# Two transformer blocks on one core: attention heads moved in among the memory's projections, the memory's norm moved ahead of a gated unit's second half, two weight splits shared with ScalarE

## The chip, the cores and the metric

One Trainium2 chip, one core of it. The metric is the device time of one execution in microseconds. A core has a matrix engine (TensorE, PE in the profile, with its weight loads as PEld), VectorE (DVE), ScalarE (ACT), GpSimd (POOL) and SyncE (SP), which here issues the transfers of the weights. Each engine runs its own list of instructions in order, and semaphores tie the lists together.

## The reference, cut to what matters

`x` is 256 tokens of width 1024. A first model of two layers is followed by a second one of two layers. Only the first one's layers are touched:

```python
for l in range(2):
    h = rmsnorm(x, norm_mix[l])
    ... = split(h @ w_in[l])
    y_ssm = s5_mixer(...)      # z = gelu(y) @ w_glu: z_out * sigmoid(z_gate)
    y_mla = mla_mixer(...)     # 8 causal heads, q and k of 64+32, v of 64; then @ mla_w_o
    y_hg  = hgrn2_mixer(...)   # 4 heads, norm, gate; then @ hg_w_o
    merged = gate0 * y_ssm + gate1 * y_mla + gate2 * y_hg
    x = x + merged @ w_out[l]
    x = x + memory_cross_attention(rmsnorm(x, norm_cross[l]), rmsnorm(mem, norm_mem[l]),
                                   x_w_q[l], x_w_kv[l], x_w_o[l])
    x = x + swiglu_ffn(rmsnorm(x, norm_ffn[l]), ...)
```

`mem` is 256 rows of width 1024 and doesn't depend on `x`. Its norm and its projections `x_w_kv` (512 columns of keys, 512 of values) can run anywhere before the cross attention.

## The kernel before

The program is written as one function per engine, each a list in order. Two things set the order around the change: TensorE's list, and the transfers of weights, which SyncE issues in the order in which TensorE asks for chunks.

*Weights in chunks.* `chunk` stands for 512 KB of a weight matrix (128 partitions x 1024 fp32). Raw chunks land in a ring `W` of four slots (`RSLOTS`), and the transfer of chunk n waits for the release of chunk n - 4. Where a product is done in split precision (`product`, L400, three products of high and low parts for one), a chunk needs a high part `WH` and a low part `WL`, in rings of three slots (`HSLOTS`). A part written for split m waits until TensorE has used split m - 3. The word `low` says who makes them: with "dve" ScalarE makes the high part and VectorE the low part, with "pool" ScalarE the high part and POOL the low part, with "both" POOL makes the one after the other (`both_parts`). Inputs of such a product are split too (`HTH` and `HTL`, for `hg_w_o` `oHG`).

*Who makes splits when.* `split_to(n)` on an engine makes its parts of all splits below n that it has not made. `split_before[name]` is the number of splits that TensorE has asked for when it ends the group of that name; `ahead(name)` is that number and up to two more (`AHEAD`), as far as the raw ring allows. Evictions (`evict`, `high_of`, `low_of`, `row_max`) call it before they wait for their bank, so that weights are made ahead.

*Banks.* A group of products has one of 8 PSUM banks (`begin`, `end`), dealt out in turn, those of open groups left out. The next user of a bank waits until an engine has freed it (`free_after`).

*The stretch of the change in TensorE's list, in each layer.* The second half of the gated unit, `glu(1)`: groups `("glu", l, 1, 1, tt)`, the gate, and `("glu", l, 1, 0, tt)`, each of a plain and a split chunk. The transposes of `HV` (`hoT`). The transposes of the memory's scaled rows, `norm_T(nrm, memX)`. The product `yh` with `hg_w_o`, four wide chunks. The projections `ck` (keys, four chunks of 24 products of 256 columns) and `cv` (values, four of 12 products of 512 columns). Then the heads: turn h of eleven does the scores of head h (L585), the transposes of the probabilities of head h - 2 (L593) and the product with the values of head h - 3 (L871). Then `ym` with `mla_w_o`, in unsplit fp32, the transposes of `merged`, and `wo` with `w_out`.

*The other engines there.* ScalarE squares `ho`, evicts `qT`, does `glu_gate(1)` (the sigmoid), waits for `mem`, sums its squares (`norm_sums`), scales one half of the rows (`norm_rows`), makes the high halves of `hoT` and of the normalized memory (`norm_cols`), evicts `ck` and `cv`, and then does the heads' exponentials (`exps`, L1587) and evictions. VectorE makes `ho_ready`, does both tiles of `glu_out(1)` (product with the gate, product with `gates`: L2510, L2511), scales the other half of the memory's rows (L2038), makes low halves (L2143, L2064), `add_branch("yh")` (L2548, L2549), and then the heads' scale and mask, row maximum and division. POOL splits weights, loads `mem` (`load_mem`, L1362), and takes the norm's root (`norm_rstd`, L1298 and L1299), which both `norm_rows` wait for:

```python
split_to(split_before["glu", l, 1, 0, 1])
wait_full(pool, ("ho", l, 1))
load_mem()
split_to(split_before["glu", l, 1, 0, 1] + 1)
norm_rstd(nrm, halves=False)
```

`memX` (the memory's rows), `memSq` (their squares) and the tiles of the `hgrn2` levels share one buffer `TB`: `memX` may be loaded once level 8 has been multiplied, `memSq` written once `ho` has been.

Of the kernel before, what the change touches and what calls it, by code (L numbers as in the profile page):

```python
# [28 lines left out]
TT = S // P  # L29
DM = 1024  # L30
KT = DM // P
# [10 lines left out]
QD = NOPE + ROPE  # L42
HGH = 4
XH = 4
DFF = 2816
FT = DFF // P
THETA = 10000.0
# [19 lines left out]
def build(nc, T, out):  # L67

    with ExitStack() as ctx:
# [261 lines left out]
        def _(pe):  # L331
# [104 lines left out]
            def wide_steps(tag, wname, l, act, K, low="dve", after=None, at=0):  # L436

                ps = {(tt, h): begin(*tag, tt, h) for tt in range(TT) for h in range(2)}
                for k in range(K if after is None else K - 2):
                    n, w = chunk(tag, rows(wname, l, k, 1, 0, DM), 1, DM, low)  # L440
                    need_rows(act, k + 1)
                    for tt in range(TT):
                        for h in range(2):
                            m = product(ps[tt, h][:, :], act, w,
                                        lambda a: a[:, at + k, tt * P:tt * P + P],
                                        lambda b: b[:, 0, h * 512:h * 512 + 512], k == 0, k == K - 1)
                            if k == K - 1:
                                end(m, *tag, tt, h)
                    if k == K - 1:
                        release_with(n, (*tag, 1, 1))  # L450
                    else:
                        release(n, m)
                    yield
                if after is not None:
                    yield from last_two(tag, wname, l, act, K, ps, after, low, lambda k: at + k,
                                        lambda k: need_rows(act, k + 1))
# [66 lines left out]
            def feature_steps(tag, wname, l, act, K, c0, tiles, low="dve", kstep=2, extra=0):  # L523
# [3 lines left out]
                if extra:  # L527
                    kr = begin(*tag, "kr")
                for k0 in range(0, K, kstep):
                    n, w = chunk(tag, rows(wname, l, k0, kstep, c0, cols), kstep, cols, low)  # L530
                    need_rows(act, k0 + kstep)
                    last = k0 + kstep == K
                    for j in range(tiles):
# [159 lines left out]
            for l in range(DEPTH):  # L693
# [161 lines left out]
                norm_T(nrm, memX)  # L855
                for j in range(2):
                    freed("hoT", l, j)
                token_out_wide(("yh", l), "hg_w_o", l, oHG, 4, low="both")

                input_from("hT", nrm)  # L860
                nrm += 1
                feature_out(("ck", l), "x_w_kv", l, HT, KT, 0, 4, low="pool")
                token_out(("cv", l), "x_w_kv", l, HT, KT, 512, 512, low="pool")

                def mla_pv(h):
                    freed("mla", "t", (l, h))
# [6 lines left out]
                    if h % 2 == 1:  # L873
                        end(m, "mo", l, h // 2)

                for h in range(HEADS + 3):
                    if h < HEADS:
                        freed("qT", l, h // 2)
                        freed("kT", l, h // 2)
                        scores("mla", (l, h), qTm[0:QD, h, :], kTm[0:QD, h, :])  # L880
                    if 2 <= h < HEADS + 2:
                        pe.wait_ge(sem["probs"], probs_at["mla", l, h - 2])
                        probs_T("mla", (l, h - 2))
# [366 lines left out]
        def _(pool):  # L1250
# [114 lines left out]
            for l in range(DEPTH):  # L1365
# [17 lines left out]
                split_to(split_before["gate", l, 5, 1])  # L1383
                pool.wait_ge(sem["y_ready"], 4 * (l + 1))
                signal(halves_of(glu_half, UT, 2), "glu_halves", l + 1)
                split_to(split_before["glu", l, 1, 0, 1])
                wait_full(pool, ("ho", l, 1))
                load_mem()
                split_to(split_before["glu", l, 1, 0, 1] + 1)
                norm_rstd(nrm, halves=False)  # L1390
                nrm += 1
                split_to(split_before["cv", l, 1])
# [40 lines left out]
        def _(act):  # L1433
# [249 lines left out]
            for l in range(DEPTH):  # L1683
# [143 lines left out]
                    ins = act.activation(PB[:, tt * 512:tt * 512 + 512], bank(("ho", l, tt))[:, :], ACT.Square)  # L1827
                    signal(ins, "ho_sq", 2 * l + tt + 1)
                take_T("qT", qTm)
                glu_gate(1)  # L1830
                act.wait_ge(sem["mem_rows"], 16 * (l + 1))
                norm_sums(nrm, memX, memSq)
                norm_rows(nrm, memX, memX)
                for j in range(2):
                    high_of(2 * j, 2, "hoT", l, j, dst=oHG[0])
                norm_cols(nrm, "norm_mem", l)
                nrm += 1
                for j in range(2):
                    evict(two(ckT, j), "ck", l, j)
                for tt in range(TT):  # L1840
                    evict(cv[:, tt, :], "cv", l, tt)
                for h in range(HEADS + 3):
                    if h < HEADS:
                        exps("mla", (l, h), h)
                    if 2 <= h < HEADS + 2:
                        take_PT("mla", (l, h - 2), h - 2)
                    if h >= 4 and h % 2 == 0:
                        evict(oML[:, (h - 4) // 2, :], "mo", l, (h - 4) // 2, width=S)
                for j in range(4):
                    high_of(2 * j, 2, "mg", l, j)  # L1850
                norm_in(nrm, "norm_cross", l, ("wo", l))
# [151 lines left out]
        def _(dve):  # L2003
# [364 lines left out]
            for l in range(DEPTH):  # L2368
# [132 lines left out]
                for q in range(4):  # L2501
                    full("y", l, q)

                def glu_out(h):
                    for tt in range(TT):
                        cols = slice(h * 512, h * 512 + 512)
                        wait_freed(dve, ("glu", l, h, 1, tt))
                        name = ("glu", l, h, 0, tt)
# [17 lines left out]
                for tt in range(TT):  # L2526
# [4 lines left out]
                    free_after(tt_(o, bank(("ho", l, tt))[:, :].rearrange("p (h e) -> p h e", h=HGH), r, ALU.mult),  # L2531
                               "ho", l, tt)
                    signal(tt_(HV[:, tt, :], HV[:, tt, :], HG[:, tt, :], ALU.mult), "ho_ready", 2 * l + tt + 1)
                glu_out(1)
                norm_rows(nrm, memX, memX)
                for j in range(2):
                    low_of(2 * j, 2, "hoT", l, j, dst=oHG)
                norm_cols(nrm, "norm_mem", l)
                nrm += 1

# [240 lines left out]
```

## Time and profile before

| what | value |
|---|---|
| median of 3 runs | 1920.4 us (1919.24 to 1921.8) |
| the profiled execution | 1917.89 us, its span 1916.1 us |
| TensorE busy | 1804.5 us, 94% of the span |
| VectorE, ScalarE, POOL busy | 1232.3, 867.0, 277.2 us |
| mean granted TensorE clock | 0.979 of full |
| DMA | 274.61 MB, 143 GB/s on average |

Times in rows are in microseconds from the start of the span. A row for a stretch gives its ends, its length, then the busy us of PE, PEld, DVE, ACT and POOL, each with its number of instructions. Each engine's busy time is a share of the same span, and an engine that is busy 94% may still wait at places. The granted clock says which part of full speed the chip let TensorE have.

### The profile page before, as it was taken

What the parts mean: (1) busy time and instruction counts of PE and PEld (TensorE: products, weight loads), DVE (VectorE), ACT (ScalarE), POOL (GpSimd) and SP (SyncE); (2) the same over time, 40 slices, a digit from 0 to 9 for tenths busy, and PEclk for the clock granted to TensorE, in tenths of its full rate; (3) what the DMA queues carried; (4) which work ended last, traced back from release to release, by engine and by line L of the source; (5) the groups of instructions that cost most, each with busy time, mean ns of one, the idle gap of its engine ahead of it and who ended that gap; (6) DMA issues with size and microseconds to landing.
All of it is one profiled execution on the core that took longest, in us unless ns stands there. A gap on an engine that the chain in (4) does not pass through costs nothing.

```text
span 1916.1 us, 27084 instructions
## 1 busy us (share of the span) xinstructions
PE 1804.5 (94%) x10038; PEld 1446.3 (75%) x10038; DVE 1232.3 (64%) x1895; ACT 867.0 (45%) x1413; POOL 277.2 (14%) x274
## 2 busy tenths in 40 slices
PE   7999989989999999999888999998899999989998
PEld 6676667569998866677577998656799864779987
DVE  7996755445667893855455566565677645566775
ACT  4224444355444422444355445336555543555553
POOL 4015453020000003557012000100100000010000
PEclk9999999999999999999999999998999999799999
DMA  6444442436566444445054666431455644135554
GB/s 160 130 130 152 133 152 89 143 105 180 160 187 188 119 127 142 133 133 177 28 191 116 194 184 192 147 110 56 141 177 163 193 153 121 56 107 170 169 187 138
DMA packets 192359, 274.61 MB, mean 143 GB/s; under 512 B 25616, under 2 KB 129540, under 8 KB 192228
## 3 DMA queue, kind: packets, MB, share of 16 engines
q1 hardware_dynamic: 191364, 269.86, 46.2%
q0 software_dynamic: 864, 3.02, 0.6%
q8 instruction: 80, 1.31, 0.3%
q14 instruction: 51, 0.42, 0.1%
HBM read 271.78 MB, written 1.05 MB: 142 GB/s over the span
## 4 chain that ended last, share of the span: by engine, by line
PE 80%; DVE 7%; ACT 6%; issue 3%; SPq 1%; POOL 1%; DMA 1%; DVEq 0%; ACTq 0%; POOLq 0%
PE bank L400 46%; PE bank L398 23%; DVE WL L1165 2%; ACT WH L1452 2%; PE bank L671 1%; PE bank L585 1%; PE bank L593 1%; PE bank L1021 1%; PE bank L871 1%; PE bank L1041 1%; PE bank L488 1%; ACT HTH L1452 1%; DVE bank L2117 1%; POOL WL L1165 0%; PE bank L654 0%
## 5 line engine op out<-in xcount | busy, mean ns | idle before, releaser
L1165 DVE TENSOR_TENSOR WL<-W,WH 128x1024 fp32r<-128x1024 f32 x304 | 372.5, 1225 | 241.9 <-ACT WH L1452 233.0
L1452 ACT ACTIVATE WH<-W 128x1024 fp32r<-128x1024 f32 x328 | 347.5, 1059 | 302.3 <-PE bank L400 267.2
L400 PE MATMUL bank<-HTH,WH 128*128 128x256 f32 x1536 | 437.6, 285 | 19.6 <-DVE WL L1165 9.5
L400 PE MATMUL bank<-HTL,WH 128*128 128x256 f32 x1536 | 434.5, 283 | 0.0
L400 PE MATMUL bank<-HTH,WL 128*128 128x256 f32 x1536 | 434.5, 283 | 0.0
L400 PEld LDWEIGHTS bank<-HTH,WH 128*128 128x128 f32 x1536 | 294.5, 192 | 25.2 <-DVE WL L1165 11.8
L400 PEld LDWEIGHTS bank<-HTL,WH 128*128 128x128 f32 x1536 | 294.7, 192 | 0.1
L400 PEld LDWEIGHTS bank<-HTH,WL 128*128 128x128 f32 x1536 | 294.6, 192 | 0.0
L400 PE MATMUL bank<-WH,HTL 128*128 128x512 f32 x672 | 261.4, 406 | 0.0
L400 PE MATMUL bank<-WH,HTH 128*128 128x512 f32 x480 | 192.7, 402 | 18.5 <-POOL WL L1165 5.7
L400 PE MATMUL bank<-WL,HTH 128*128 128x512 f32 x480 | 188.5, 393 | 0.0
L398 PE MATMUL bank<-W,M 128*128 128x512 f32 (+1 forms) x416 | 166.2, 555 | 2.6 <-issue 2.6
L400 PEld LDWEIGHTS bank<-WH,HTL 128*128 128x128 f32 x672 | 127.1, 189 | 32.2 <-issue 5.3
L398 PE MATMUL bank<-W,HTF 128*128 128x512 f32 (+1 forms) x384 | 149.8, 539 | 0.0
L398 PEld LDWEIGHTS bank<-W,M 128*128 128x128 f32 x416 | 79.2, 194 | 75.7 <-issue 72.9
L400 PEld LDWEIGHTS bank<-WH,HTH 128*128 128x128 f32 x480 | 91.2, 190 | 43.8 <-POOL WL L1165 7.4
L398 PEld LDWEIGHTS bank<-W,HTF 128*128 128x128 f32 x384 | 68.2, 190 | 67.5 <-issue 66.1
L1293 POOL TENSOR_SCALAR QSQ<-QSQ 128x2 f32<-128x2 f32 x9 | 5.1, 571 | 767.4 <-ACT PB L1492 767.4
L400 PEld LDWEIGHTS bank<-WL,HTH 128*128 128x128 f32 x480 | 91.2, 190 | 18.1
L398 PE MATMUL bank<-HTF,W 128*128 128x256 f32 x448 | 99.6, 381 | 0.7 <-DVE HTF L2392 0.6
L1338 POOL TENSOR_TENSOR WL<-W,WH 128x1024 fp32r<-128x1024 f32 x40 | 97.6, 2440 | 3.2
L398 PEld LDWEIGHTS bank<-HTF,W 128*128 128x128 f32 x448 | 84.3, 190 | 13.4 <-issue 1.4
(405 smaller groups left out, 2495.8 us busy)
## 6 DMA issues: line engine op xcount, KB each, us to landing
W<-in_w_in SPq DMA_DIRECT2D x132, 512.0 KB, 3.7
W<-in_ffn_w_gate_up SPq DMA_DIRECT2D x176, 256.0 KB, 3.4
W<-in_w_up SPq DMA_DIRECT2D x176, 256.0 KB, 3.6
W<-in_ffn_w_down SPq DMA_DIRECT2D x44, 512.0 KB, 3.7
W<-in_w_down SPq DMA_DIRECT2D x44, 512.0 KB, 4.2
W<-in_w_out SPq DMA_DIRECT2D x32, 512.0 KB, 3.4
W<-in_ssm_w_glu SPq DMA_DIRECT2D x16, 512.0 KB, 4.3
W<-in_x_w_kv SPq DMA_DIRECT2D x16, 512.0 KB, 3.4
```

Of the source, the lines that this page charges most:

```text
L398: return pe.matmul(out, at_a(a), at_b(b), start=start, stop=stop, skip_group_check=True)
L400: m = pe.matmul(out, at_a(a[x]), at_b(b[y]), start=(start and i == 0), stop=(stop and i == 2), skip_group_check=True)
L488: m = pe.transpose(ps[:, k * S + tt * P:k * S + tt * P + P], X[:, tt, (2 * j + k) * P:(2 * j + k) * P + P], IDENT[:, :])
L585: ins = pe.matmul(ps[:, tt * S:tt * S + S], qT[:, tt * P:tt * P + P], kT, start=(tt == 0), stop=(tt == TT - 1), skip_group_check=True)
L593: ins = pe.transpose(ps[:, kt * S + tt * P:kt * S + tt * P + P], p_buf(tag, m[1])[:, tt, kt * P:kt * P + P], IDENT[:, :])
L671: m = pe.matmul(ps[:, h * P:h * P + P], ka[:, h, b * P:b * P + P], qa[:, h, b * P:b * P + P], start=(h == 0), stop=(h == HGH - 1), skip_gr ...
L871: m = pe.matmul(ps[64 * (h % 2):64 * (h % 2) + 64, 0:S], vtok[:, kt, h * VD:h * VD + VD], PT[h % 2][:, kt, :], start=(kt == 0), stop=(kt = ...
L1021: pe.matmul(ps[:, tt * S:tt * S + S], qkT[r:r + 64, h // 2, tt * P:tt * P + P], qkT[r:r + 64, 4 + h // 4, :], start=(tt == 0), stop=False, ...
L1041: m = pe.matmul(ps[:, h * HD:h * HD + HD], t_buf("a2", h)[:, kt, tt * P:tt * P + P], proj2[:, kt, 640 + (h // 4) * HD:640 + (h // 4) * HD ...
L1165: eng.tensor_tensor(WL[:, m % HSLOTS, 0:width], W[:, n % RSLOTS, 0:width], h, ALU.subtract)\
L1338: signal(pool.tensor_tensor(low, raw, high.bitcast(F32), ALU.subtract), s, v)
L1452: copy = lambda dst, src, scale=1.0: act.activation(dst, src, ACT.Copy, scale=scale)
```

## The change

Three edits, the same in both layers of the first model.

1. *The heads.* TensorE's `ck` and `cv` steps are made one iterator `memory` of eight chunks. Two run ahead of the heads, the other six in turns 0, 1, 3, 5, 7 and 9 (`MEM_STEPS`), behind that turn's scores. ScalarE evicts `ck` in turn 1 behind the exponentials and `cv` behind the last turn, and asks for its parts of the splits ahead of each head's exponentials. The first two `ck` chunks get their low parts from VectorE instead of POOL.
2. *The memory's norm.* POOL loads `mem` when level 8 is done, ahead of the split of the (1, 0) chunk, and takes the root ahead of the first `hg_w_o` chunk. ScalarE sums the squares ahead of `glu_gate(1)`. VectorE scales its rows ahead of `glu_out(1)` and makes the low halves of `hoT` between that one's two tiles.
3. *The splits of `hg_w_o`.* Of the last two of the four chunks ScalarE makes the high part, one behind the first four columns of the memory's high halves and one behind the last four.

```diff
+MEM_STEPS = (0, 1, 3, 5, 7, 9)
...
# TensorE
-                token_out_wide(("yh", l), "hg_w_o", l, oHG, 4, low="both")
+                token_out_wide(("yh", l), "hg_w_o", l, oHG, 4, low=("both", "both", "pool", "pool"))
...
-                feature_out(("ck", l), "x_w_kv", l, HT, KT, 0, 4, low="pool")
-                token_out(("cv", l), "x_w_kv", l, HT, KT, 512, 512, low="pool")
+                memory = itertools.chain(feature_steps(("ck", l), "x_w_kv", l, HT, KT, 0, 4,
+                                                       low=("dve", "dve", "pool", "pool")),
+                                         token_steps(("cv", l), "x_w_kv", l, HT, KT, 512, 512, low="pool"))
...
+                next(memory)
+                next(memory)
                 for h in range(HEADS + 3):
                     if h < HEADS:
                         ...
                         scores("mla", (l, h), qTm[0:QD, h, :], kTm[0:QD, h, :])
+                    if h in MEM_STEPS:
+                        next(memory)
# POOL
-                split_to(split_before["glu", l, 1, 0, 1])
-                wait_full(pool, ("ho", l, 1))
-                load_mem()
-                split_to(split_before["glu", l, 1, 0, 1] + 1)
+                split_to(split_before["glu", l, 1, 1, 1])
+                wait_full(pool, ("lev", l, 8, 0))
+                load_mem()
+                split_to(split_before["glu", l, 1, 0, 1])
                 norm_rstd(nrm, halves=False)
# ScalarE
-                glu_gate(1)
                 act.wait_ge(sem["mem_rows"], 16 * (l + 1))
                 norm_sums(nrm, memX, memSq)
+                glu_gate(1)
                 norm_rows(nrm, memX, memX)
                 for j in range(2):
                     high_of(2 * j, 2, "hoT", l, j, dst=oHG[0])
-                norm_cols(nrm, "norm_mem", l)
+                last_yh = split_before["yh", l, 1, 1]
+                high_cols(nrm, "norm_mem", l, 0, 4)
+                split_to(last_yh - 1)
+                high_cols(nrm, "norm_mem", l, 4, KT)
+                split_to(last_yh)
                 nrm += 1
-                for j in range(2):
-                    evict(two(ckT, j), "ck", l, j)
-                for tt in range(TT):
-                    evict(cv[:, tt, :], "cv", l, tt)
                 for h in range(HEADS + 3):
                     if h < HEADS:
+                        split_to(ahead(("mla", "s", (l, h))))
                         exps("mla", (l, h), h)
+                    if h == MEM_STEPS[1]:
+                        for j in range(2):
+                            evict(two(ckT, j), "ck", l, j)
                     ...
+                for tt in range(TT):
+                    evict(cv[:, tt, :], "cv", l, tt)
# VectorE
-                glu_out(1)
                 norm_rows(nrm, memX, memX)
+                glu_out(1, (0,))
                 for j in range(2):
                     low_of(2 * j, 2, "hoT", l, j, dst=oHG)
+                glu_out(1, (1,))
                 norm_cols(nrm, "norm_mem", l)
```

`glu_out` takes the tiles it is to do as a second argument, and `wide_steps` and `feature_steps` take a tuple for `low`, one word a chunk.

## Rows read from the trace of the kernel before

**Rows 1.** the page's busy times: engine, us, share, instructions

```profile
PE 1804.5 (94%) x10038; PEld 1446.3 (75%) x10038; DVE 1232.3 (64%) x1895; ACT 867.0 (45%) x1413; POOL 277.2 (14%) x274
```

**Rows 2.** stretches of layers 0 and 1: length, busy us (count), clock, DMA share, GB/s

```profile
267.80:277.48 9.68, 4.92 (x26) 4.30 (x25) 9.40 (x9) 4.91 (x10) 7.12 (x4) 0.71 0.60 213
277.48:288.90 11.42, 11.42 (x49) 9.35 (x48) 5.09 (x9) 3.29 (x5) 7.07 (x4) 0.94 0.22 67
288.90:311.48 22.58, 22.58 (x146) 20.69 (x145) 9.99 (x7) 8.16 (x9) 15.71 (x7) 1.00 0.56 184
311.48:340.19 28.71, 22.94 (x96) 14.10 (x96) 18.00 (x40) 17.81 (x46) 0.00 (x0) 0.88 0.00 1
...
873.80:881.20 7.40, 3.93 (x26) 3.34 (x25) 7.16 (x8) 4.52 (x9) 7.17 (x4) 0.89 0.63 229
881.20:915.50 34.30, 34.30 (x194) 30.25 (x194) 15.15 (x16) 11.95 (x15) 23.07 (x11) 0.97 0.49 154
915.50:944.27 28.77, 22.99 (x96) 14.20 (x96) 18.00 (x40) 17.81 (x46) 0.00 (x0) 0.88 0.00 0
```

**Rows 3.** TensorE's timeline, layer 0: start, us, line, operation, tiles, count, idle before

```profile
248.68 1.06 PE L677 MATMUL bank<-TB 128*128 128x128 f32 x8
...
267.81 1.03 PE L689 MATMUL bank<-IDENT,HV 128*128 128x128 f32 x8
273.04 1.94 PE L564 MATMUL bank<-IDENT,TB 128*128 128x128 f32 x8 [4.20 <-issue]
```

**Rows 4.** VectorE's timeline, layer 0, and one row of layer 1

```profile
266.74 0.69 DVE L2510 TENSOR_TENSOR XN<-bank,PB 128x512 f32<-128x512 f32 x1 [5.46 <-PE bank L400]
267.47 1.54 DVE L2511 TENSOR_TENSOR XN<-XN,A 128x512 f32<-128x512 f32 x1
...
271.80 3.63 DVE L2038 TENSOR_SCALAR TB<-TB,RSTD 128x512 f32<-128x512 f32 x2
...
873.47 0.69 DVE L2511 TENSOR_TENSOR XN<-XN,A 128x512 f32<-128x512 f32 x1
```

**Rows 5.** ScalarE's timeline, layer 0

```profile
260.54 0.60 ACT L1553 ACTIVATE PB<-bank 128x512 f32<-128x512 f32 x1 [3.49 <-PE bank L400]
...
262.55 1.06 ACT L1482 ACTIVATE TB<-TB 128x1024 f32<-128x1024 f32 x1
...
267.45 1.48 ACT L1452 ACTIVATE TB<-TB,RSTD 128x512 f32<-128x512 f32 x2 [2.57 <-POOL RSTD L1299]
...
283.74 1.06 ACT L1452 ACTIVATE WH<-W 128x1024 fp32r<-128x1024 f32 x1 [5.02 <-PE bank L400]
```

**Rows 6.** POOL's timeline, layer 0, and the transfer of `mem`: KB, us to landing

```profile
254.50 0.97 POOL L1362 DMA_DIRECT2D TB<-in_mem  x1 [1.36 <-PE bank L825]
262.71 1.03 POOL L1336 CAST WH<-W 128x1024 fp32r<-128x1024 f32 x1 [7.24 <-DMA W<-in_hg_w_o]
263.83 2.38 POOL L1338 TENSOR_TENSOR WL<-W,WH 128x1024 fp32r<-128x1024 f32 x1
...
266.62 0.73 POOL L1299 TENSOR_TENSOR RSTD<-SSQ,NHALF 128x2 f32<-128x2 f32 x1
...
TB<-in_mem POOLq DMA_DIRECT2D x1, 1024.0 KB, 5.6
```

**Rows 7.** TensorE in the heads: its longest wait, two turns' scores

```profile
PE bank L593 <- DVE PB L2203: 3.5, 1, 3.5
...
323.08 1.15 PE L585 MATMUL bank<-TB 96*128 96x256 f32 x4
...
325.61 1.13 PE L585 MATMUL bank<-TB 96*128 96x256 f32 x4
```

**Rows 8.** ScalarE's first exponential; VectorE's sums from 281 to 300, by form

```profile
313.95 1.28 ACT L1587 ACT_TABLE_LOAD   x1 [1.78 <-DVE NMX L2191]
315.25 0.51 ACT L1587 ACTIVATE PB<-PB,NMX 128x256 f32<-128x256 f32 x1
...
L2549 DVE TENSOR_TENSOR XN<-XN,A 128x512 f32<-128x512 f32 x4 | 9.0, 2244 | 0.1
```

More of the change, by code:

```diff
@@ L439, in wide_steps @@
                 for k in range(K if after is None else K - 2):
-                    n, w = chunk(tag, rows(wname, l, k, 1, 0, DM), 1, DM, low)
+                    n, w = chunk(tag, rows(wname, l, k, 1, 0, DM), 1, DM,
+                                 low[k] if isinstance(low, tuple) else low)
                     need_rows(act, k + 1)
@@ L529, in feature_steps @@
                 for k0 in range(0, K, kstep):
-                    n, w = chunk(tag, rows(wname, l, k0, kstep, c0, cols), kstep, cols, low)
+                    n, w = chunk(tag, rows(wname, l, k0, kstep, c0, cols), kstep, cols,
+                                 low[k0 // kstep] if isinstance(low, tuple) else low)
                     need_rows(act, k0 + kstep)
@@ L2502, in _, with glu_out @@
                     full("y", l, q)
-                def glu_out(h):
-                    for tt in range(TT):
+                def glu_out(h, tts=range(TT)):
+                    for tt in tts:
                         cols = slice(h * 512, h * 512 + 512)
```

## The prediction

> **What bounds the kernel now.** I read the page first. TensorE is busy for 94% of the span [rows 1], so time can only come from places where it stands or runs at half clock, or from fewer products; the change removes no product. Then I cut the stretch that the diff touches into stages [rows 2]. There are two such stretches, one a layer. In each, TensorE is busy for 4.92 of 9.68 us (layer 0) and 3.93 of 7.40 us (layer 1) between the gated unit and the `hg_w_o` product, is full through the `hg_w_o` product and the memory's projections, and is busy for 22.94 of 28.71 us and 22.99 of 28.77 us in the eight attention heads. There its granted clock is 0.88 on average, a mixture of the 2.4 GHz and the 1.2 GHz level. Those two holes are what the change works on.
>
> *The first hole.* TensorE ends the transposes of `hoT` at 268.8 and does the first transposes of `memX` at 273.04 [rows 3]. It waits for the scaled rows of the memory. Working back: VectorE scales its half only from 271.80 on, in 3.63 us, because both tiles of `glu_out(1)` stand ahead of it [rows 4]. ScalarE scales its half at 267.45, having waited 2.57 us for POOL's root at 266.62 to 267.35 [rows 5, 6]. That root stands on POOL behind the 3.5 us split of the first `hg_w_o` chunk [rows 6], and the sums behind it start only at 262.55, after `glu_gate(1)` [rows 5].
>
> *The second hole.* With nothing but heads on TensorE, a head's scores wait for VectorE's row maximum, ScalarE's exponentials and VectorE's division. The first division alone holds TensorE for 3.5 us [rows 7]. Where nothing waits and the clock is full, one head's turn is 325.61 - 323.08 = 2.53 us [rows 7]. Eight are 20.2 us, against 28.7 us taken.
>
> **The change, part by part.** All against the profiled execution: 1917.89 us, of which the span is 1916.1. The median shown is 1920.4, or 2.5 above it, and I add that at the end.
>
> *Memory's norm earlier.* POOL issues the load of `mem` after level 8 (TensorE does it from 248.68 to 249.7 [rows 3]) and ahead of one more chunk's split instead of at 254.50. POOL has finished the (1,1) chunk's split by then. The issue takes 0.97 us [rows 6], so the (1,0) chunk's split ends about 1 us later, near 254.3. Its reader on TensorE comes some 3 us before the 267.81 of `hoT`, so this is hidden. The transfer takes 5.6 us [rows 6]: it is there at about 256. ScalarE comes to the sums when `qT` is evicted, at 260.54 - 3.49 = 257.05, and does them in 267.45 - 2.57 - 262.55 = 2.3 us [rows 5]. `glu_gate(1)` behind them is not late, its bank is full at 260.5. POOL's root is then ready at about 260.4, in front of the `hg_w_o` split, which begins when its data lands at 262.71 [rows 6]. VectorE, idle from 266.74 - 5.46 = 261.3 [rows 4], scales its rows until about 263, ScalarE after the gate until 264.1. Both are done before TensorE reaches the transposes at 268.8. These end at 268.8 + 1.8 = 270.5, sixteen at the pace of the eight of `hoT`, 0.11 each [rows 3].
>
> *What is late next.* The `hg_w_o` product needs the low half of `hoT` and a bank that `glu_out(1)`'s second tile frees. VectorE: first tile 0.69, its product with the gates 1.54 (as now, POOL splitting beside it), two low halves 0.7 each as other 128x512 operations, then 0.69 for the bank [rows 4]. From 266.74 this ends at 271.1; with semaphores 271.3, where TensorE starts the product now at 277.48. Layer 1's VectorE does its first product with the gates at 873.47 instead of 267.47, 606.0 later [rows 4], so the start is 877.3 instead of 881.2. At full clock the product is 11.42 x 0.94 = 10.7; I take 10.9. It ends at 282.2 instead of 288.9: 6.7 us in layer 0. In layer 1 the same way 3.9, and 0.3 for its clock of 0.97 instead of 1.00 over the first part: 4.2.
>
> *Do the splits keep up?* ScalarE now makes the high halves of `yh` chunks 2 and 3. A high half takes 1.06 us, a low half on POOL 2.38 [rows 5, 6], against 3.5 on POOL alone for both. By ScalarE's order (two `hoT` halves until 269.8, four columns of 0.5 us, since 128x1024 takes 1.06, then the high half) chunk 2's high half is ready at 272.9 and its low half at 275.3. TensorE wants it at 271.3 + 2 x 10.9 / 4 = 276.8. Chunk 3: 276.0, 278.4, wanted at 279.5. Each has about 1 us in hand. Chunks 0 and 1 of `ck` are split by ScalarE and VectorE by 279.2 and 281.9, wanted at 282.2 and 285.1. No stall, little slack.
>
> *Heads among the projections.* The eight projection chunks took 22.58 us [rows 2], 2.82 each, and stay. Two run before the first head, six inside the eleven turns. TensorE's load from the end of `yh` is 22.6 + 20.2 (heads at 2.53) + 0.8 for the eviction of the last output, as now. Waits: the first head's chain starts on VectorE with `add_branch("yh")`. Today it takes 4 x (0.69 + 2.24) = 12 us with the gaps, since its sum of two SBUF tiles takes 2.24 us beside POOL's splits [rows 8]; such an operation takes 0.69 without [rows 4]. From 282.0 the new one meets two of POOL's splits, not four, and I get 290.9. Row maximum 1.4 (two operations on 128x512), table load and exponentials 1.28 + 1.25 (two of 0.51 with their sums) [rows 8], one high half, the second head's exponentials, another high half, two evictions of `ck`: 299.2. The evictions free the bank in which `cv` begins. TensorE stands there from about 298.1: 1.1 us. After that a head's chain (maximum 1.4, exponentials 1.25, division 0.9, eviction 0.6) has two turns and a projection step, some 7.9 us, to run in. The high halves are asked for two chunks ahead. I see no further wait.
> So 282.2 + 22.6 + 20.2 + 0.8 + 1.1 = 326.9, where `ym` starts at 340.19 now: 13.3 us in layer 0. The middle alone is 51.3 - 44.7 = 6.6. In layer 1: 4.2 + 6.6 = 10.8.
>
> *The rest.* The `cv` evictions move behind the last head (1.2 us of ScalarE under `ym`'s 11.4), the fourth `ym` bank is one of them and is wanted last: nothing. The `w_out` transfer behind `ym` waits for `ym`'s own releases as before: nothing gained or lost.
>
> **Sum.** 13.3 + 10.8 = 24.1 less. I take 23, since several steps have under 1 us in hand. 1917.9 - 23 = 1894.9, and with the 2.5: **1897.4 us**. Its own range is 1889 to 1904: at best no wait and TensorE straight from the transposes into `yh`, 2 x (1.1 + 0.9) + 24.1 = 28 and 3 more for heads whose loads overlap the projections; at worst `add_branch("yh")` keeps its 12 us, 3 us a layer on the chain, and one us more.
>
> **Two rules.** The row of the table load shows 1.28 us and the exponential 0.02 us behind it, ScalarE having been idle [rows 8]. The Trainium skill, ScalarE: Activation LUTs, What ACT_TABLE_LOAD costs, gives about 1.38 us of drain besides for each change of set. By the row nothing is to be added; by the page `cv` would begin 1.4 us later in each layer, and the sum would be 21.3. The trace does not bear it out.
> The Trainium skill, SBUF — State Buffer, Who interferes with whom, speaks against this change: a VectorE operation with two SBUF inputs and a GpSimd operation fully block each other. The trace agrees, with the 2.24 against 0.69 us above. The third rival is what it would do to the heads.
>
> **The rivals.**
> 1. *Only the front gains* (chance 0.10). The heads' chain is the limit with or without company, each step of TensorE waits for it, and the eleven turns take the 51.3 us that they and the projections take now. Then 6.7 + 4.2 = 10.9 less: 1909.5. For it: the heads use 17.8 us of ScalarE and 18.0 of VectorE in 28.7 [rows 2], and ScalarE gets highs and evictions besides. Against: loads of both engines are under 80% of 44.7.
> 2. *Only the heads gain* (0.07). The memory's sums come late, because `mem` lands late or the root waits, and TensorE starts `yh` when it does now. 2 x 6.6 = 13.2 less: 1907.2. Against: the load has 1 us in hand at 256, and 5 more before the transposes.
> 3. *VectorE blocked by POOL in the heads* (0.11). Divisions and sums now run beside the four low halves of `cv`. Scaling rows of 128x512 took 3.63 for two beside POOL [rows 4]. At most each low half blocks for its whole 2.4 us on the path: 4 x 2.4 = 9.6 a layer, so 24.1 - 19.2 = 4.9 less, 1915.5; half of that is likelier, 1906. Against: division has several us in hand after the second head.
> 4. *A ring of waits, slower* (0.05). ScalarE's highs stand behind exponentials, these wait for maxima, these for scores, which TensorE does only behind the step that needs the high. If the two chunks ahead did not cover it, each step would pay scores 0.9, maximum 1.4, exponentials 1.25, high 1.06, low 2.4, step 2.8 = 9.8. The two `ck` steps have 5.3 of TensorE's own work in that time, the four `cv` steps 7.9, so 2 x 4.5 + 4 x 1.9 = 16.6 more a layer. 44.7 + 16.6 is 10.0 above the 51.3, so 20.0 slower less 10.9: 9 us slower, 1929. It decides from 12 us of stalls a layer on. Against it: the order written for ScalarE asks two ahead, and the raw chunks come early.
> The likeliest case keeps 0.67.
>
> **The range and the chances.** 1889 to 1910 takes in the likeliest, rivals 1 and 2 and the milder half of 3, with under 2 in 10 outside. Within 0.2% (3.8 us) is what a measurement can't tell from no change. Faster 0.92; the same 0.03 (the far end of rival 3); slower 0.05.
>
> **What would show it.** In the profile after: POOL's root before its first `hg_w_o` split; under 1.5 us between the `hoT` and the `memX` transposes' end and the product, no 4 us hole; the two `yh` chunks' highs on ScalarE and `yh` at an even 2.73 us a chunk; clock 1.00 through the heads; `add_branch("yh")` in about 9 us; one wait of about 1 us at the first `cv` step; 45 us from the end of `yh` to `ym`. It would be wrong if TensorE's waits for divisions or for low halves inside the turns came to more than 3 us a layer, or if a stage behind `ym` took longer than before.

## The result, and the profile after

The changed kernel takes 1896.87 us (median of 4 runs, 1893.49 to 1899.83) against 1919.82 for the kernel before (median of 4). The ratio is 0.9888, with a 95% interval of 0.9872 to 0.9903: 23 us less. The forecast was 1897.4. The execution that was profiled is the slowest of the four, 1899.83 us.

The page's busy times of the changed kernel, as [rows 1]:

```profile
PE 1798.9 (95%) x10038; PEld 1445.6 (76%) x10038; DVE 1233.6 (65%) x1899; ACT 872.4 (46%) x1417; POOL 264.2 (14%) x266
```

The two stretches of the changed kernel, cut at the same events as [rows 2]: from the transposes of `hoT` to the start of `yh`, to the end of `yh`, to the start of `ym`; the first three rows are layer 0, the others layer 1.

```profile
267.39:271.24 3.85, 2.78 (x25) 2.56 (x24) 2.68 (x5) 3.00 (x6) 2.56 (x1) 1.00 0.87 310
271.24:282.25 11.01, 11.01 (x49) 9.09 (x49) 6.75 (x12) 6.26 (x9) 4.82 (x2) 1.00 0.52 162
282.25:327.50 45.25, 42.62 (x241) 33.35 (x240) 29.75 (x48) 25.07 (x54) 14.28 (x6) 1.00 0.27 88
862.91:867.97 5.06, 2.79 (x26) 2.57 (x24) 4.92 (x5) 4.15 (x7) 2.02 (x1) 1.00 0.87 300
867.97:880.54 12.57, 12.57 (x48) 10.25 (x49) 6.50 (x11) 5.09 (x7) 4.91 (x2) 0.86 0.37 112
880.54:925.90 45.36, 42.36 (x241) 33.42 (x240) 29.68 (x49) 25.23 (x54) 14.30 (x6) 1.00 0.27 89
```

The reader is to see three things. The last stretch of each layer, projections and heads together, fell from 51.3 us (22.58 + 28.71, [rows 2]) to 45.25 and 45.36, and its clock is 1.00 throughout where the heads had 0.88. The front of layer 0, from `hoT` to the end of `yh`, fell from 288.90 - 267.81 = 21.09 to 14.86. The front of layer 1 fell only from 19.10 (873.81 to 892.91) to 17.63, and the clock of its `yh` is 0.86.

What held layer 1's front: VectorE's timeline, then POOL's, then TensorE's, of the changed kernel.

```profile
862.57 2.90 DVE L2530 TENSOR_TENSOR XN<-XN,A 128x512 f32<-128x512 f32 x1
...
866.96 0.69 DVE L2529 TENSOR_TENSOR XN<-bank,PB 128x512 f32<-128x512 f32 x1
```

```profile
862.55 2.38 POOL L1348 TENSOR_TENSOR WL<-W,WH 128x1024 fp32r<-128x1024 f32 x1
```

```profile
867.97 0.47 PE L401 MATMUL bank<-WH,OTR 128*128 128x512 f32 x1 [2.27 <-DVE XN L2529]
```

VectorE's product with the gates started 0.02 us behind POOL's difference and took 2.90 us. The low halves of `hoT` and the freeing of the second bank stood behind it, and TensorE idled 2.27 us and then ran part of `yh` at the lower clock. Of the 2.77 us by which this front is longer than layer 0's, 1.21 is the later start (5.06 against 3.85) and 1.56 the lower clock (12.57 against 11.01).

In layer 0 the same two operations came in the other order, VectorE's first, and VectorE's took 0.69 us. It then waited 1.06 us for ScalarE's high half of `hoT` all the same:

```profile
267.03 0.69 DVE L2530 TENSOR_TENSOR XN<-XN,A 128x512 f32<-128x512 f32 x1
268.78 1.42 DVE L2162 TENSOR_TENSOR OTR<-bank,OTR 128x512 fp32r<-128x512 f32 x2 [1.06 <-ACT OTR L1462]
```

```profile
267.23 2.73 POOL L1348 TENSOR_TENSOR WL<-W,WH 128x1024 fp32r<-128x1024 f32 x1
```

What waits of TensorE's are left in layer 0's stretch (engine and line that waited, releaser, us in total, times, longest), against the 3.5 us of [rows 7] and the 4.20 us of [rows 3]:

```profile
PE bank L401 <- ACT M L1563: 1.2, 1, 1.2
...
PE bank L401 <- issue: 1.1, 1, 1.1
PE bank L399 <- issue: 0.8, 1, 0.8
PE bank L875 <- ACT PB L1563: 0.7, 1, 0.7
```

The first is the eviction of `ck` ahead of the first `cv` step, the second the start of `yh`, the third the last output before `ym`, the fourth an eviction of transposed probabilities.

### The profile page after: what moved, and what is told of

Its sections match the earlier page's. It is cut to its first block, busy times and chain, and to the rows that moved or that the text cites. A ratio compares the mean times of both kernels' runs of the same rounds, so it can differ in the third digit from the quotient of the medians.

```text
span 1898.0 us, 27088 instructions
## 1 busy us (share of the span) xinstructions
PE 1798.9 (95%) x10038; PEld 1445.6 (76%) x10038; DVE 1233.6 (65%) x1899; ACT 872.4 (46%) x1417; POOL 264.2 (14%) x266
## 4 chain that ended last, share of the span: by engine, by line
PE 81%; DVE 8%; ACT 5%; issue 2%; SPq 1%; POOL 1%; DMA 0%; DVEq 0%; ACTq 0%; POOLq 0%
PE bank L401 47%; PE bank L399 24%; DVE WL L1175 2%; ACT WH L1462 2%; PE bank L674 2%; PE bank L588 1%; PE bank L596 1%; PE bank L1031 1%; PE bank L875 1%; PE bank L1051 1%; PE bank L490 1%; ACT HTH L1462 1%; DVE bank L2136 1%; DVE HTL L2083 1%; POOL WL L1175 1%
## 5 line engine op out<-in xcount | busy, mean ns | idle before, releaser
L1175 DVE TENSOR_TENSOR WL<-W,WH 128x1024 fp32r<-128x1024 f32 x308 | 377.5, 1226 | 254.0 <-ACT WH L1462 245.2
L1462 ACT ACTIVATE WH<-W 128x1024 fp32r<-128x1024 f32 x332 | 352.3, 1061 | 288.7 <-PE bank L401 255.6
L401 PE MATMUL bank<-WH,HTH 128*128 128x512 f32 x480 | 194.7, 406 | 21.1 <-POOL WL L1175 5.7
L401 PEld LDWEIGHTS bank<-WL,HTH 128*128 128x128 f32 x480 | 91.8, 191 | 18.1
L1348 POOL TENSOR_TENSOR WL<-W,WH 128x1024 fp32r<-128x1024 f32 x36 | 87.9, 2441 | 2.9
```

What stands on the lines that cost most here:

```text
L401: m = pe.matmul(out, at_a(a[x]), at_b(b[y]), start=(start and i == 0), stop=(stop and i == 2), skip_group_check=True)
L1175: eng.tensor_tensor(WL[:, m % HSLOTS, 0:width], W[:, n % RSLOTS, 0:width], h, ALU.subtract)\
L1348: signal(pool.tensor_tensor(low, raw, high.bitcast(F32), ALU.subtract), s, v)
L1462: copy = lambda dst, src, scale=1.0: act.activation(dst, src, ACT.Copy, scale=scale)
```

## The experiments

Each kernel was timed beside the kernel before in five rounds. Since runs of one kernel spread over up to 13 us (e7), the stretches of the traces say more than the ratios. Two lengths are used throughout: the *front*, from the first transpose of `hoT` to the end of `yh`, and the *middle*, from there to the start of `ym`, each for both layers. For the kernel before they are 21.1 and 19.1, and 51.3 and 51.4; for the changed kernel 14.9 and 17.6, and 45.3 and 45.4.

**e1_heads_only.** Edits 2 and 3 undone.

```diff
# against the changed kernel
-                token_out_wide(("yh", l), "hg_w_o", l, oHG, 4, low=("both", "both", "pool", "pool"))
+                token_out_wide(("yh", l), "hg_w_o", l, oHG, 4, low="both")
# POOL
-                split_to(split_before["glu", l, 1, 1, 1])
-                wait_full(pool, ("lev", l, 8, 0))
+                split_to(split_before["glu", l, 1, 0, 1])
+                wait_full(pool, ("ho", l, 1))
                 load_mem()
-                split_to(split_before["glu", l, 1, 0, 1])
+                split_to(split_before["glu", l, 1, 0, 1] + 1)
# ScalarE: glu_gate(1) ahead of norm_sums, norm_cols without the splits between
# VectorE: glu_out(1) ahead of norm_rows
```

> The heads among the projections alone; the memory's norm, the order of the gated unit's second half and the splits of hg_w_o stay as in the kernel before. Theory of the prediction (the two holes are separate and add up): the front keeps its 9.7 and 7.4 us between 267.8 and 277.5 and between 873.8 and 881.2, and the stretch from the end of yh to ym falls from 51.3 to about 45 us a layer as in the changed kernel (282.5 to 327.5): 12 to 13 us less than before, ratio about 0.993 to 0.994. Rival (only the front gains, the heads merely profit from VectorE and ScalarE being ahead after an earlier front): under 4 us less. Second rival (the heads are worth nearly all): 18 us or more less.

Measured: 1908.11 us against 1916.63, ratio 0.9959 (0.9944 to 0.9974), 8 us less. Windows of the trace, as above:

```profile
267.09:276.21 9.12, 4.58 (x25) 3.96 (x24) 8.88 (x8) 4.39 (x9) 6.91 (x4) 0.76 0.58 203
276.21:288.36 12.15, 12.15 (x50) 9.95 (x49) 6.12 (x11) 3.60 (x6) 3.44 (x2) 0.90 0.30 95
288.36:333.60 45.24, 42.60 (x241) 33.35 (x240) 29.78 (x48) 25.05 (x54) 14.30 (x6) 1.00 0.26 86
866.49:875.45 8.96, 3.71 (x26) 3.25 (x24) 8.72 (x8) 4.24 (x8) 6.75 (x4) 0.84 0.60 215
875.45:888.30 12.85, 12.85 (x51) 10.43 (x50) 6.12 (x11) 3.60 (x6) 3.45 (x2) 0.85 0.27 86
888.30:933.50 45.20, 42.37 (x241) 33.43 (x240) 29.71 (x48) 25.04 (x54) 14.24 (x6) 1.00 0.27 87
```

The middle is 45.2 in both layers without any of the front's edits: 12.2 us less, as expected. The whole is less than 12 and misses the expected ratio of 0.993 to 0.994, since the front, whose code is that of the kernel before, took 21.3 and 21.8 us here. The 19.1 of layer 1 before is the short case of it, the other three lie at 21.1 to 21.8: there VectorE's two products with the gates took 0.69 us each, in layer 1 of e1 1.16 and 2.00. The rival that only the front gains is out.

**e2_front_only.** Edit 1 undone.

```diff
-MEM_STEPS = (0, 1, 3, 5, 7, 9)
+MEM_STEPS = ()
...
-                                                       low=("dve", "dve", "pool", "pool")),
+                                                       low="pool"),
...
-                next(memory)
-                next(memory)
+                for _ in memory:
+                    pass
# ScalarE evicts ck and cv ahead of the heads
```

> The memory's norm moved and the splits of hg_w_o shared, with all eight projection chunks ahead of the heads and split by POOL as before. Theory of the prediction: 10.9 us less than before by the prediction's sum; with what the changed kernel's trace shows (6.3 us earlier start of yh in layer 0, some 2 to 2.5 in layer 1, where VectorE's product with the gates takes 2.9 us beside POOL) 8 to 9.5 us less, and the heads keep 28.7 us with a clock near 0.88. Rival (VectorE's add_branch beside POOL's six splits is late and eats the gain before the heads): 3 to 5 us less. The sum of this run's gain and that of the heads alone should be the whole gain within 3 us; more than that apart would mean that the edits depend on each other.

Measured: 1910.13 against 1916.63, ratio 0.9955 (0.9939 to 0.9971), 7 to 9 us less. Windows of layer 0:

```profile
269.89:273.74 3.85, 2.78 (x26) 2.57 (x24) 2.72 (x5) 3.00 (x6) 2.59 (x1) 1.00 0.87 296
273.74:284.74 11.00, 11.00 (x49) 9.09 (x50) 6.02 (x11) 6.25 (x9) 8.44 (x4) 1.00 0.44 148
284.74:335.80 51.06, 45.30 (x241) 34.73 (x240) 27.98 (x47) 25.98 (x55) 15.71 (x7) 0.93 0.24 81
```

The front is 14.9 us, and 14.8 in layer 1, where VectorE's product was not held up this time. The middle stays at 51.1 and 50.8. By the traces the edits don't depend on each other: the stretches of each alone add to those of both, 12.2 and 10.5 us. By time this is not shown. The medians of the two parts give 8.5 and 6.5 us, together 8 less than the 23 of both, and the expectation called anything over 3 apart a sign of dependence; by the ratios it is 5. I go by the traces, since each interval is about 3 us to either side.

No run separates the two halves of edit 1, the steps between the heads and the low parts of the first two `ck` chunks on VectorE. Nor are the four moves of edit 2 (load, root, sums, VectorE's order) taken apart.

**e3_pool_alone.** Edit 3 undone, the rest as changed.

```diff
-                token_out_wide(("yh", l), "hg_w_o", l, oHG, 4, low=("both", "both", "pool", "pool"))
+                token_out_wide(("yh", l), "hg_w_o", l, oHG, 4, low="both")
# ScalarE
-                high_cols(nrm, "norm_mem", l, 0, 4)
-                split_to(last_yh - 1)
-                high_cols(nrm, "norm_mem", l, 4, KT)
-                split_to(last_yh)
+                norm_cols(nrm, "norm_mem", l)
```

> The changed kernel with all four chunks of hg_w_o split by POOL alone, as before, everything else as changed. If sharing them with ScalarE is needed: POOL takes 1.04 + 2.4 us and the gaps, 3.6 us a chunk, from 262.3 on; chunk 2 would be ready at about 273.7, chunk 3 must wait for the release of chunk 0 at 274.0 and is ready at 277.6, before TensorE wants it at about 279.4. So by this count little is lost: 0 to 1 us slower than the changed kernel, and the third edit is worth next to nothing. Rival (contention: POOL's cast and difference are stretched while VectorE does its products and its columns): chunk 3 is late by 1 to 3 us in each layer, 2 to 6 us slower than the changed kernel.

Measured: 1897.55, ratio 0.9899 (0.9881 to 0.9917), the changed kernel's time. `yh` takes 10.96 and 11.00 us, the middle 45.2. The two high halves on ScalarE are worth nothing here, as POOL alone is in time: in layer 0 its last low half ended at 279.75, and at 2.75 us a chunk TensorE came to it at 273.09 + 3 x 2.75 = 281.3. In this run it was layer 0 whose front was held (15.9 us, the first product with the gates 2.80), and layer 1 was not (14.85). TensorE idled 2.17 us there, and its clock stayed at 1.00; that is why this hold cost 1.1 us and the one above 2.8.

**e4_gates_later.** VectorE frees both banks of the gated unit first and does the products with the gates behind the low halves of `hoT`.

```diff
                 norm_rows(nrm, memX, memX)
-                glu_out(1, (0,))
+                glu_out(1, parts=(0,))       # banks times the sigmoid, both tiles
                 for j in range(2):
                     low_of(2 * j, 2, "hoT", l, j, dst=oHG)
-                glu_out(1, (1,))
+                glu_out(1, parts=(1,))       # products with the gates, both tiles
```

> The changed kernel with VectorE's two products with the gates moved behind the low halves of hoT: both banks of the gated unit are freed first. In the changed kernel yh starts at 271.24 and 867.97 because VectorE does a product with the gates first, 0.69 us in layer 0 but 2.90 in layer 1, where it stands against POOL's difference, and TensorE idles 1.1 and 2.3 us with half clock behind it in layer 1 (18.5 us for 96 products against 16.9). Theory: layer 1's shortfall is that one blocked operation. Then yh starts about 1.0 us earlier in layer 0 and 2.0 in layer 1, with up to 1.5 more from the clock: 2.5 to 4.5 us less than the changed kernel. Rival (the product with the gates is only pushed into the low columns and add_branch, and the columns become late for the ck chunks): no change.

Measured: 1898.35, ratio 0.9902 (0.9888 to 0.9917), by the median no gain over the changed kernel. The windows of both layers from `hoT` to the start of `yh`:

```profile
266.60:269.66 3.06, 2.78 (x25) 2.57 (x24) 2.29 (x4) 2.24 (x5) 2.28 (x1) 1.00 0.88 327
...
861.58:864.64 3.06, 2.78 (x25) 2.57 (x24) 2.29 (x4) 2.23 (x5) 2.35 (x1) 1.00 0.91 337
```

3.06 us in both against 3.85 and 5.06, and `yh` at full clock in both: the front is 14.05 us. So the blocked product was the whole shortfall of layer 1, 17.63 - 14.86 = 2.8 us, and the free one costs another 0.8. That the timing doesn't show these 4.4 us is put down to the spread; no run shows it: the unchanged part behind layer 1's `ym` took 973.1 us here and 972.1 in the trace of the changed kernel, and the parts between the layers differ by a few us from trace to trace.

**e5_changed_again.** The changed kernel, unaltered.

> The changed kernel, unaltered, beside the others of this call on one chip. From the end of yh to ym 45.2 to 45.4 us in both layers, as in four traces so far. From the transposes of hoT to the end of yh 14.9 us in a layer where VectorE's first product with the gates is not held up, and 15.9 to 17.6 where it starts beside a difference on POOL; which of the two a layer gets is open. 18 to 24 us less than before.

Measured: 1896.92 against 1919.22, ratio 0.9891 (0.9871 to 0.9912). Front 14.84 and 14.82, middle 45.26 and 45.23. A layer's front is mostly free: of twelve fronts in the six traces with this order of VectorE's (the changed kernel twice, e2, e3, e6 and e7) three were held, to 15.9, 15.9 and 17.6 us. Of eight in the four traces with the later products (e4, e8, e9, e10) none was.

**e6_evict_first.** `ck` is evicted ahead of the `cv` high half.

```diff
                     if h == MEM_STEPS[1]:
                         for j in range(2):
-                            evict(two(ckT, j), "ck", l, j)
+                            evict(two(ckT, j), "ck", l, j, split=False)
```

> The changed kernel with ScalarE evicting ck ahead of the high half of the cv chunk that it made first. In the changed kernel the first cv step waits 1.2 and 1.4 us for that eviction. Theory: the wait is this one high half of 1.06 us in a chain, so TensorE starts cv about 1.0 us earlier in each layer and the stretch from the end of yh to ym is 44.2 instead of 45.3. Rival (the next wait takes its place: the second head's division, which POOL holds up until 301.3, and the values' product 0.7 us behind it): 45.2 as before, with a longer wait at the transposes of the second head's probabilities.

Measured: 1901.86, ratio 0.9902 (0.9881 to 0.9924). By time nothing is gained: the median is 5 us above that of e5 on the same chip, with the ranges of both overlapping. In the traces the untouched part behind layer 1's `ym` is 4.4 us longer here, 976.3 against 971.9. The middle's windows of both layers:

```profile
281.76:325.90 44.14, 42.56 (x241) 33.36 (x240) 27.74 (x48) 25.11 (x54) 14.29 (x6) 1.00 0.27 92
874.95:919.08 44.13, 42.37 (x241) 33.45 (x240) 27.67 (x49) 25.10 (x54) 14.32 (x6) 1.00 0.27 90
```

1.1 and 1.2 us less. The eviction's wait is gone, but a wait of 0.8 and 1.0 us for that chunk's low half on POOL stands in its place, so the first `cv` step comes only 0.4 us earlier in each layer (16.56 us behind the end of `yh` in layer 0 against 16.98), not the 1.0 that the theory had. The other 0.7 us is the wait for an eviction of probabilities, which is gone: the second head's division took 0.94 us for both tiles instead of 3.03. In the changed kernel POOL's second `cv` difference followed the first at once and held it until 301.29; here it started at 299.42, behind the division's end. The number was right, and the reason only in part. The rival, that this division takes over, is out.

**e7_cv_dve.** VectorE makes the low halves of `cv`.

```diff
-                                         token_steps(("cv", l), "x_w_kv", l, HT, KT, 512, 512, low="pool"))
+                                         token_steps(("cv", l), "x_w_kv", l, HT, KT, 512, 512, low="dve"))
```

> The changed kernel with the low halves of the four cv chunks made by VectorE (1.23 us each) instead of POOL (2.4 us each), so that POOL does nothing during the turns of the heads. Theory (POOL's blocks are absorbed: in the changed kernel one division takes 2.5 us longer and another 1.0 longer, yet TensorE waits only 0.7 us for what hangs on them): the divisions take 0.36 us a tile throughout, TensorE's 0.7 us wait goes, and the stretch from the end of yh to ym stays within 1 us of 45.3, since VectorE carries 4.9 us more. Rival (the blocks cost what they last, 3.5 us a layer): the stretch falls to 42 to 43 us, 5 us or more less than the changed kernel.

Measured: 1904.28, ratio 0.9924 (0.9903 to 0.9944). The middle is 50.3 and 49.1 us, 5 and 4 more than in the changed kernel, where both expectations had it equal or shorter. VectorE's timeline of this kernel:

```profile
292.10 0.69 DVE L2210 TENSOR_REDUCE NMX<-PB 128x2 f32<-128x512 f32 x1
296.59 1.23 DVE L1175 TENSOR_TENSOR WL<-W,WH 128x1024 fp32r<-128x1024 f32 x1 [3.80 <-ACT WH L1462]
297.85 0.69 DVE L2207 SCALAR_TENSOR_TENSOR PB<-bank,MASK 128x512 f32<-128x512 f32 x1
...
301.79 1.23 DVE L1175 TENSOR_TENSOR WL<-W,WH 128x1024 fp32r<-128x1024 f32 x1 [1.54 <-ACT WH L1462]
```

TensorE's longest wait there:

```profile
PE bank L596 <- DVE PB L2222: 3.4, 1, 3.4
```

This is the ring of the fourth rival, closed by another edge. `row_max` on VectorE asks for its low halves two chunks ahead. The low half needs ScalarE's high half, which stands behind the first head's exponentials. So the second head's maximum, free of any need of that chunk, waits for the first head's exponentials. VectorE idles 3.80 us, and in all 8.4 us for highs in layer 0's middle. TensorE's waits there go from 1.9 to 4.0 us; the rest, 2.9 us, is TensorE busy for longer (45.48 against 42.62 us), at a clock of 0.93 behind its wait of 3.4 us. The divisions themselves take 0.354 us a tile throughout, against 0.640 and 0.474 on average in the changed kernel, which does show that POOL's differences are what stretches them. The price of that stretching can't be read from this kernel, since the ring hides it.

**e8_gates_evict.** Both small edits, e4 and e6.

> The changed kernel with both small edits: both products with the gates behind the low halves of hoT, and ck evicted ahead of the cv chunk's high half. From hoT to the end of yh 14.05 us in both layers, never blocked. If the eviction is worth its 1 us, the stretch to ym is 44.2 in both. Against the changed kernel of this call 1.6 us less without its blocks and 2 to 5 with them, and 2 more for the eviction.

Measured: 1893.51 (1892.35 to 1894.14), ratio 0.9865 (0.9846 to 0.9883). Front 14.03 and 14.06, middle 44.14 and 44.29. All its four runs lie below all six of e5 on the same chip (1894.26 to 1903.55).

**e9_cv_high_early.** Besides, the first `cv` chunk's high half ahead of the first exponentials.

```diff
                     if h < HEADS:
-                        split_to(ahead(("mla", "s", (l, h))))
+                        split_to(ahead(("mla", "s", (l, h))) + (h == 0))
                         exps("mla", (l, h), h)
```

> The kernel with both small edits, and besides ScalarE makes the high half of the first cv chunk ahead of the first head's exponentials, where it stood idle for 6 us, instead of behind them. In the kernel with both edits TensorE's first cv step waits 0.8 and 1.0 us for that chunk's low half. Theory (a chain of high, low, step): the wait goes and the second head's exponentials come 1.06 us earlier; from the end of yh to ym 43.2 instead of 44.2, 2 us less in all. Rival (POOL's difference now runs beside add_branch's last sum or the first division, blocks VectorE there, and the row maxima come later): 44.2 or more.

Measured: 1893.79, ratio 0.9862 (0.9844 to 0.9881), the same as e10 on the same chip. The middle is 44.5 and 44.6 us, not 43.2. TensorE's longest wait in it, layer 0:

```profile
PE bank L596 <- DVE PB L2222: 1.4, 1, 1.4
```

The wait for the low half is gone, and one for the first division stands in its place. It is the rival as written: POOL's difference, now at 289.32, ran beside `add_branch`'s last sum, which took 2.14 us and not 0.69, and the row maxima came later by that much.

```profile
290.13 2.14 DVE L2571 TENSOR_TENSOR XN<-XN,A 128x512 f32<-128x512 f32 x1
```

**e10_gates_evict_again.** The kernel of e8 once more.

> The kernel with both small edits once more, beside the one above on one chip: 14.05 us from hoT to the end of yh, 44.2 from there to ym, in both layers; 25 to 28 us less than before.

Measured: 1894.04 against 1922.04, ratio 0.9858 (0.9838 to 0.9877). Front 14.06 twice, middle 44.1 and 44.3. In its two measurements this version is 26 and 28 us below the kernel before, the fastest beside e5 to e7 and level with e9. Against the changed kernel its traces show 2 x 0.8 + 2 x 1.1 = 3.8 us less and no held front. The ratios of the two kernels to the one before overlap at their intervals' edges, so the step from the changed kernel to it rests on the traces and on the separate runs of e8 and e5, 3.4 us apart by their medians.

## Why the prediction was right

*The start of `yh`.* Forecast 271.3 in layer 0, measured 271.24. The memory's root came at 259.44, ahead of the first `hg_w_o` split at 262.25, and TensorE did the transposes straight behind those of `hoT`. What it waited for next was what the prediction named, VectorE's freeing of the second bank. That the number agrees to 0.1 us is luck, though. The prediction had the first product with the gates at 1.54 us and no wait behind it; measured are 0.69 and a wait of 1.06 for ScalarE's high half of `hoT`, which it left out, with a start 0.44 us earlier. Also, [rows 2] cut the kernel before at 277.48, while the first product of its `yh` started at 277.14:

```profile
277.14 0.77 PE L400 MATMUL bank<-WH,OTR 128*128 128x512 f32 x1
```

So its `yh` took 11.76 us and not the 11.42 that the prediction scaled. The gain over the whole front doesn't hang on that cut.

*`yh` itself.* Forecast 10.9 us, measured 11.0. That sharing the splits was needed for it is wrong: e3 has the same 11.0 without. The prediction compared 1.06 + 2.38 with 3.5 us of POOL, but never asked when POOL alone would be late.

*Projections and heads.* Forecast 44.7 us, measured 45.25. `add_branch("yh")` was to end 8.9 us after its start and took 282.24 to 290.99, 8.75 us, with two sums held by POOL's two splits (2.29 and 2.09) and two free at 0.69. The `ck` evictions were to end at 299.2 and did at 299.76. The wait ahead of `cv` was 1.2 us for a forecast of 1.1. The 0.7 us for an eviction of probabilities in turn 4 was missed: it hangs on the second head's division, one tile of which took 2.44 us beside POOL, and it is absent in e6, where that division took 0.94 for both tiles. Of layer 0's gain of 6.0 us, 3.1 is less waiting and 2.9 is TensorE busy for less long, 42.62 against 22.58 + 22.94, at a clock of 1.00 where the heads had 0.88. So rival 3's mechanism is there, and costs 0.7 us of the up to 9.6 a layer.

*The term that was mis-sized* is the front of layer 1: forecast 4.2 us less. The profiled execution has 1.5, and e5, e2 and e6, where VectorE was not held, 4.3. The prediction allowed the product with the gates 1.54 us in both layers and the full clock behind it. Measured, it takes 0.69 (once 0.87) or, held up, 2.80 to 2.90; and in the profiled execution the lower clock behind the longer wait took 1.6 us more. A second small miss is the middle: 6.0 and not 6.6 less in each layer.

*The signs.* The root came before the first `hg_w_o` split, and `yh` ran at 2.75 us a chunk. The wait behind the `memX` transposes was under 1.5 us in layer 0 (1.08) but not in layer 1 (2.27). Behind `ym` nothing grew: from its start to the transposes behind `wo` it is 39.58 us against 39.56 before in layer 0, and from layer 1's `ym` to the end 972.1 against 971.8.

*The sum.* Traces without a held front give 6.2 + 4.3 + 2 x 6.05 = 22.6 us, against the 24.1 of the sum, the 23 taken from it, and the measured 23. The profiled execution itself has only 6.2 + 1.5 + 6.0 + 6.0 = 19.7 in these stretches and 18.1 in its span. The agreement with the measured 23 is partly luck: the four medians of the kernel before, from one set of runs to the next, lie between 1916.63 and 1922.04.

*The rivals.* Only the front (e1 shows the middle falling alone), only the heads (e2 shows the front falling alone) and the slower ring in the changed kernel are out. The ring is real, though: e7 closed it and lost 9 us of the gain in the two middles. The prediction had the edge wrong. It looked for it in TensorE's steps, where the look-ahead of two covers it; it lies in that same look-ahead, on an engine that both feeds the chain and helps with the splits.

*The rule on the table load.* The first exponential came at 293.81, behind a load of 1.28 us from 292.51, no later. The highs between the exponentials caused no further load. The Trainium skill, ScalarE: Activation LUTs, What ACT_TABLE_LOAD costs, adds a drain of about 1.38 us; no such time stands in these rows, and the row was right to go by here.

## What to carry to other kernels

Where an engine is kept waiting by a latency-bound chain, put independent work of the same engine into its turns: here six chunks of 2.8 us in each layer took 12 us of waits and lower clock away in all, while the chain itself was left as it was. Then read which look-ahead stands in front of which link. A prefetch that is harmless on one engine closes a ring on another. And cost each stage by its lengths in several traces: the middle repeated to 0.2 us (45.2 to 45.4 in five traces) where whole runs differed by up to 13, and where a stage didn't repeat, as the front, the rows named the operation that was held.

## What the runs showed of the hardware

*Who starts first.* A VectorE operation with two SBUF inputs takes 0.69 us, or waits for POOL's difference to end first: 2.90 us when it started 0.02 us behind one. The same program had its front held in layer 1 in one trace and in neither layer in another. In the twelve fronts with this order of VectorE's, the three held ones are those where POOL's difference had started first, by 0.02, 0.12 and 0.11 us (the changed kernel, e3, e7). In the nine others VectorE's product had started first, by 0.01 to 0.41 us, and POOL's difference took 2.70 to 2.91 us instead of 2.37 or 2.38. The Trainium skill, SBUF — State Buffer, Who interferes with whom, states that a VectorE instruction with two SBUF inputs contends with a GpSimd instruction that reads SBUF, and that issue order decides who blocks. These rows agree with it. The divisions, with one SBUF input, were held as well: 0.35 us a tile free, up to 2.44 beside POOL's difference.

*The clock in untouched stretches.* The times of one kernel follow its mean granted clock. The changed kernel's four runs have 0.982, 0.983, 0.987 and 0.983 beside 1899.83, 1896.26, 1893.49 and 1897.47 us, and the six of e6 go from 0.983 at 1893.52 to 0.978 at 1903.5. Part of it lies in places that the change doesn't touch: the window from 1489 to 1510 of the changed kernel has 0.92, the one at the same work of the kernel before, the second row, 1.00.

```profile
1489.00:1510.00 21.00, 20.68 (x84) 16.97 (x85) 13.01 (x16) 10.07 (x14) 0.00 (x0) 0.92 0.61 201
1507.00:1527.00 20.00, 19.83 (x87) 16.41 (x88) 13.31 (x17) 10.60 (x15) 0.00 (x0) 1.00 0.65 212
```

The loss is nearly all in the first 4 us, where the clock is 0.59, and TensorE had just stood idle for a low half of VectorE's:

```profile
1489.32 0.50 PE L401 MATMUL bank<-WH,MH 128*128 128x512 f32 x1 [1.82 <-DVE WL L1175]
```

In the kernel before, the longest such wait there is 1.5 us. But a wait alone doesn't settle it: the clock fell behind 1.82 us here and behind 2.27 in layer 1's front, and stayed at 1.00 behind 2.17 in the held front of e3. What decides was not tried.
